# Grouped matmuls in the joined units, four banks for the SSD decays, an earlier SSD tail, half-loaded first units and a per-token final norm

## The reference

```
for i in range(2):
    x = x + 0.5 * swiglu(rmsnorm(x, ffn_norm[i, 0]), w_gate_up[i, 0], w_down[i, 0])
    h = rmsnorm(x, mix_norm[i])
    y = short_conv_mixer(h, ...) if i == 0 else ssd_mixer(h, ...)
    x = x + y
    x = x + memory_cross_attn(rmsnorm(x, xa_norm[i]), rmsnorm(mem, xa_mem_norm[i]), ...)   # 4 heads, 256 memory tokens
    x = x + 0.5 * swiglu(rmsnorm(x, ffn_norm[i, 1]), w_gate_up[i, 1], w_down[i, 1])
return rmsnorm(x, final_norm)
```

## Time and profile before

| | before |
|---|---|
| device time, median of 3 runs (range) | 1339.04 us (1337.76 to 1341.26) |
| device time of the profiled execution | 1343.49 us |
| span of the profiled execution | 1341.7 us |
| PE busy | 1294.3 us (96%) |
| PEld busy | 1169.4 us (87%) |
| DVE busy | 1002.5 us (75%) |
| ACT busy | 756.5 us (56%) |
| POOL busy | 231.6 us (17%) |
| share of the chain that ended last: PE, DVE, ACT | 79%, 10%, 5% |
| granted TensorE clock, mean | 0.991 |

### The profile page before, as it was taken

One profiled execution on the slowest core, in us unless ns is written; L12 is line 12 of the kernel. 1 busy time (PEld: TensorE's weight loads), 2 busy tenths in 40 slices (PEclk: granted clock), 3 DMA queues, 4 the chain that ended last, 5 costly groups with the idle time before them and its releaser, 6 DMA issues.

```text
span 1341.7 us, 24083 instructions
## 1 busy us (share of the span) xinstructions
PE 1294.3 (96%) x8324; PEld 1169.4 (87%) x8324; DVE 1002.5 (75%) x1553; ACT 756.5 (56%) x1362; POOL 231.6 (17%) x316
## 2 busy tenths in 40 slices
PE   6999999999999999999999997999979999999996
PEld 5888889989998888888888885899979999888885
DVE  6887767687768888668887666798856767888764
ACT  6555544356556556446555554678855655655641
POOL 2333111112001111101111100024451201111111
PEclk9999999999999999999999999999999999999998
DMA  6656655545445556645556443344344543555750
GB/s 241 192 187 205 199 167 171 183 157 186 129 142 181 188 183 218 195 146 178 183 187 230 166 167 126 123 149 138 126 142 170 164 149 133 186 182 186 225 192 32
DMA packets 60120, 228.32 MB, mean 170 GB/s; under 512 B 6673, under 2 KB 7953, under 8 KB 59793
## 3 DMA queue, kind: packets, MB, share of 16 engines
q1 hardware_dynamic: 60048, 227.39, 51.8%
HBM read 226.31 MB, written 1.05 MB: 169 GB/s over the span
## 4 chain that ended last, share of the span: by engine, by line
PE 79%; DVE 10%; ACT 5%; issue 3%; POOL 2%; DMA 0%; DVEq 0%; ACTq 0%; SPq 0%; POOLq 0%
PE bank L1175 79%; DVE w_lo L673 3%; ACT w_hi L343 3%; DVE acc L676 2%; DVE decay L943 1%; DVE acc L673 1%; DVE x L673 1%; ACT sq L376 1%; ACT corr L343 1%; POOL ssq L1087 0%; DVE t L673 0%; ACT h L343 0%; POOL y L1156 0%; DMA x<-x_t 0%; POOL root_y L1138 0%
## 5 line engine op out<-in xcount | busy, mean ns | idle before, releaser
L1175 PE MATMUL bank<-h,w_hi 128*128 128x512 f32 (+1 forms) x2056 | 621.3, 365 | 15.5 <-DVE w_lo L673 10.3
L673 DVE TENSOR_TENSOR w_lo<-raw,w_hi 128x1024 fp32r<-128x1024 f32 (+1 forms) x401 | 521.6, 1304 | 54.2 <-ACT w_hi L343 52.7
L1175 PE MATMUL bank<-h,w_lo 128*128 128x256 f32 x1736 | 489.3, 282 | 0.0
L343 ACT ACTIVATE w_hi<-raw 128x1024 fp32r<-128x1024 f32 (+1 forms) x401 | 442.1, 1103 | 45.3 <-PE bank L1175 44.1
L1175 PE MATMUL bank<-a,w_hi 128*128 128x512 f32 (+1 forms) x1664 | 461.2, 348 | 0.2 <-DVE w_lo L673 0.2
L1175 PEld LDWEIGHTS bank<-h,w_hi 128*128 128x128 f32 x2056 | 367.7, 190 | 83.7 <-issue 10.2
L1175 PE MATMUL bank<-a,w_lo 128*128 128x256 f32 x1280 | 360.8, 282 | 0.0
L1175 PEld LDWEIGHTS bank<-h,w_lo 128*128 128x128 f32 x1736 | 330.4, 190 | 0.0
L1175 PEld LDWEIGHTS bank<-a,w_hi 128*128 128x128 f32 x1664 | 290.1, 191 | 42.3 <-issue 0.5
L1175 PEld LDWEIGHTS bank<-a,w_lo 128*128 128x128 f32 x1280 | 243.8, 190 | 0.0
L343 ACT ACTIVATE corr<-bank 128x256 f32<-128x256 f32 x233 | 88.5, 381 | 267.6 <-PE bank L1175 267.6
(11 more groups left out here) (177 smaller groups left out, 1115.6 us busy)
## 6 DMA issues: line engine op xcount, KB each, us to landing
raw<-w_gu SPq DMA_DIRECT2D x176, 512.0 KB, 3.6
raw<-w_down SPq DMA_DIRECT2D x64, 704.0 KB, 4.1
raw<-w_xbc SPq DMA_DIRECT2D x32, 512.0 KB, 3.5
raw<-w_conv_in SPq DMA_DIRECT2D x24, 512.0 KB, 4.1
raw<-w_q SPq DMA_DIRECT2D x16, 512.0 KB, 4.2
raw<-w_k SPq DMA_DIRECT2D x16, 512.0 KB, 4.2
raw<-w_v SPq DMA_DIRECT2D x16, 512.0 KB, 3.6
raw<-w_o SPq DMA_DIRECT2D x16, 512.0 KB, 3.7
```

The lines of the kernel that those rows point to most:

```text
L343: return nc.scalar.activation(out, in_, ACT.Copy, scale=scale)
L673: return nc.vector.tensor_tensor(out, a, b, op)
L1175: return nc.tensor.matmul(out, lhs, rhs, start=start, stop=stop, skip_group_check=check)
```

## The change

Five things are changed.

1. **Order in a joined unit.** `pairs` now takes a range of blocks: first the 512-column matmuls of all of them, then the 256-column ones. Number and shapes stay.
2. **Decays.** Four banks (5, 6, 4, 7) take the place of two, PE's wait is for `diff_ready` j-3, ACT's exps of a step are those of the diffs of the step before, `rows` is finished before the two small exps, and `normed_lo` moves from DVE to POOL.
3. **Tail of the SSD scan.** The formulas become a table (`due`) with exceptions for groups 5 to 7 (`TAIL`), and part of the last eight units is issued ahead of and behind group 7's transposes (`second_halves`).
4. **Start.** x comes in five pieces, the first two units in halves (`half_units`), unit 0 by ACT's queue; five matmuls on `ones` run first; the first norm's sums come after four units, and its root is spread after a fifth; `mem` is loaded later and in four pieces.
5. **End.** x times the final gain is transposed as each tile comes (`turn_final`), and the root is applied per token (per partition) in four 512-column operations by DVE and ACT; four transfers of 256 KB go out in place of eight of 128 KB.

```diff
+HALF_W = UNIT_W // 2
+X_CHUNKS = [(0, 1), (1, 2), (2, 4), (4, 6), (6, 8)]
...
+        DECAY_BANKS = (5, 6, 4, 7)
...
-        SSD_STEPS = 4 * (GROUPS + 3) + 2
         SSD_UNITS = 4 * GROUPS + KT
+        SSD_STEPS = SSD_UNITS + 2
+
+        TAIL = {"y": {7: 35}, "state": {7: 36}, "y_add": {7: 36}, "yo": {6: 34, 7: 36}, "yoff": {6: 35, 7: 37},
+                "square": {6: 36, 7: 38}, "root": {6: 36, 7: 38}, "yn": {5: 35, 6: 37, 7: 39}, "yt": {5: 35, 6: 38, 7: 40}, "a_rest": {5: 36, 6: 39, 7: 40}}
...
         def _(act):
...
+                if f == 0:
+                    corr_copy(0, 0, n0)
+                    corr_copy(1, 1, n0 + 1)
+                    split(n0 + 1 + AHEAD)
+                    for t in range(2, 4):
+                        act.wait_ge(evac[t - 2], 1)
+                        corr_copy(t, t, n0 + t)
+                    split(n0 + 2 + AHEAD)
+                    norm(0)
+                    ffn_post(f, 0, 0, 0, None)
+                    ffn_post(f, 1, 1, 0, a_hi[:, 0, :])
+                    ffn_post(f, 2, 2, 0, None)
...
                         copy(rows[:, :], bank[7][:, 0:SEQ]).then_inc(row_hi, 1)
+                        act.wait_ge(row_rest, 1)
+                        copy(rows[0:2 * H, :], acc[0][0:2 * H, :]).then_inc(row_lo, 1)
                         nc.scalar.activation(e_acum[:, :], d["nacum"][:, 1, :], ACT.Exp, scale=-1.0).then_inc(acum_exp, 1)
                         nc.scalar.activation(dsd[:, :], rest[:, :], ACT.Exp).then_inc(acum_exp, 1)
-                        act.wait_ge(row_rest, 1)
-                        copy(rows[0:2 * H, :], acc[0][0:2 * H, :]).then_inc(row_lo, 1)
...
-                    while lcount < decays_by(s - 1):
+                    while lcount < decays_by(s - 2):
                         decays(lcount)
...
         def _(dve):
...
-                    if 5 < s <= 5 + KT:
-                        normed_lo(s - 6)
...
+            dve.wait_ge(rms_n_ready, SS_INDEX[NORM_FINAL] + 1)
+            dve.wait_ge(turned, 1)
+            for c in range(2):
+                cols = slice(c * 512, c * 512 + 512)
+                nc.vector.tensor_scalar(final[:, 0, cols], bank[FINAL_BANKS[0][c]][:, :], rms_n[:, 0:1], None, ALU.mult).then_inc(out_ready, 1)
...
         def _(pool):
...
+                for k in range(KT):
+                    pool.wait_ge(nhi_ready, k + 1)
+                    nc.gpsimd.tensor_tensor(a_lo[:, H_NORMED + k, :], normed[k], a_hi[:, H_NORMED + k, :].bitcast(F32), ALU.subtract).then_inc(nh_ready, 1)
...
         def _(pe):
...
-            def pairs(out, lh, ll, both, start, stop):
-
-                mm(out[:, :], lh, both, start, False)
-                return mm(out[:, SEQ:], ll, both[:, 0], False, stop)
+            def pairs(out, s, r, ks, k0, start, stop, ready=None):
+
+                for k in ks:
+                    if ready:
+                        pe.wait_ge(*ready(k))
+                    mm(out[:, :], w_hi[s][:, k * P:k * P + P], r[:, :, k0 + k, :], start and k == ks[0], False)
+                for k in ks:
+                    ins = mm(out[:, SEQ:], w_lo[s][:, k * P:k * P + P], r[:, 0, k0 + k, :], False, stop and k == ks[-1])
+                return ins
...
+                if b == 0:
+                    half_units()
+                    one_unit(2, bank[2], KT, 0, h, True, True)
+                    one_unit(3, bank[3], KT, 0, h, True, True)
+                    norm_sums(b)
+                    one_unit(4, free(name, 4), KT, 0, h, True, True)
+                    pe.wait_ge(eye_in, 16)
+                    norm_spread(b)
+                    for t in range(5, 8):
+                        one_unit(t, free(name, t), KT, 0, h, True, True)
+                    return
...
-                at_least(pe, diff_ready, j - 1)
+                at_least(pe, diff_ready, j - 3)
...
-                    ins = mm(bank[5 + j % 2][:, r * SEQ:r * SEQ + SEQ], pick[:, hd:hd + 1].broadcast_to((P, P)), rows[:, :], True, True)
+                    ins = mm(bank[DECAY_BANKS[j % 4]][:, r * SEQ:r * SEQ + SEQ], pick[:, hd:hd + 1].broadcast_to((P, P)), rows[:, :], True, True)
...
+                    if t == SSD_UNITS:
+                        second_halves(range(1), range(KT - 2))
...
+                second_halves(range(1, 3), range(KT - 2))
+                second_halves(range(3), range(KT - 2, KT))
+                second_halves(range(3, KT), range(KT))
...
+            for k in range(KT - 1):
+                turn_final(k)
             norm_sums(NORM_FINAL)
-            norm_spread(NORM_FINAL)
+            turn_final(KT - 1).then_inc(turned, 1)
```

More of the change, by code:

```diff
@@ L317, in load_phase @@
                 else:
-                    with sp.Fori(1, units // SLOTS) as i:
+                    with sp.Fori(3 if name == "gu0" else 1, units // SLOTS) as i:
                         for s in range(SLOTS):
@@ L1408, in wide_unit, with second_halves @@
                     ins.then_inc(unit_done, 1)
+            def second_halves(ks, part):
+                for k in ks:
+                    out = bank[k] if k < 4 else free("ssd_out", k)
+                    unit(first["xbc"] + SSD_UNITS + k, half(out, k), KT, KT, a, False, True,
+                         ready=(yt_ready, 0) if k == 0 else None, check=True, part=part)
             def ssd():
@@ L1505, in ssd @@
                         ins.then_inc(xt_done, 1)
-                for k in range(KT):
-                    out = bank[k] if k < 4 else free("ssd_out", k)
-                    unit(nx + SSD_UNITS + k, half(out, k), KT, KT, a, False, True,
-                         ready=(yt_ready, 0) if k == 0 else None, check=True)
+                second_halves(range(1, 3), range(KT - 2))
+                second_halves(range(3), range(KT - 2, KT))
+                second_halves(range(3, KT), range(KT))
             pe.wait_ge(ones_set, 1)
-            pe.wait_ge(gain_in, 16)
+            for i in range(5):
+                mm(bank[7][:, 0:SEQ], ones[:, :], ones[:, 0:1].broadcast_to((P, SEQ)), True, True)
             ffn(0)
```

302 lines of the change are left out of this document (188 added, 114 removed).

## The result

The changed kernel took 1319.92 us (median of 4 runs, 1319.54 to 1320.69) beside 1340.15 us (1337.76 to 1341.81) for the kernel before: a ratio of 0.985, with a 95% interval of 0.9833 to 0.9867. It is 20 us faster. The forecast was 1304 with a range from 1295 to 1317: the direction was right, the time lies 3 us above the range, and of 34.8 us forecast 20.2 came.

What follows compares the result with a forecast made beforehand. PE was taken to bound the kernel. Grouping -10.5, decays -15, SSD tail -9, start +1, openings +1.2 and end -2.5 sum to -34.8, from a median of 1339.04 to 1304 us; 8 in 10 from 1295 to 1317.

Steps and rivals of the forecast that it cites:

- What bounds the kernel: Whole kernel: PE, busy 96% of a 1341.7 us span and 79% of the chain, so time comes only from PE.
- Decays: Ten z steps: exp leaves the ring, PE sets the step, 47.7 us towards 31.0; -15 us (-16.7 to -9).
- rival (b): z steps: POOL slows two DVE operations, DVE becomes the limit; -9 in place of -15, 1310 us; chance 0.13.
- Grouping: Joined units: a wide and narrow pair falls from 0.3535 to 0.3487 us, 2200 pairs; -10.5 us (-15 to -2).
- the openings: Openings of gu1 to gu3: narrow matmuls come behind the last wide one while PE waits for h; +1.2 us (0 to 2.5).
- the bound set: Sign in gu, down and o units: a whole grouped unit of eight blocks at 2.79 us or less is right.
- SSD tail: SSD scan's end: group 7's 7.83 us stall and half clock go, group 5 stalls 1.5; -9 us (-10.5 to -7.5).
- Start: Kernel start: first matmul 3.3 us earlier, but norm sums and root later, unit 6 near 31.8; +1 us (-1.5 to +3.5).
- End: Output: root used at once, fewer wider operations on DVE and ACT, doubled transfers; -2.5 us (-3.2 to -1.8).
- Rival (a): Joined units: matmul order is worth nothing, the pair stays at 0.354 us; 1315 us; chance 0.22.

Runs made afterwards that it cites:

- the third: Repaired kernel (three repairs to the changed kernel, 1308.4 us) with grouped units two by two, two wide matmuls then two narrow: 1307.2 us (1306.4 to 1308.0).

## Why the prediction was wrong, step by step

**What bounds the kernel: right.** Every gain and loss was one of PE's stretches.

**Decays: right.** -15 forecast (-16.7 at best), -16.4 in the phase and -17.1 measured alone. PE sets the step and DVE does not; the fear that POOL would slow it there (rival (b)) did not come true, and the move of `normed_lo` was needed for nothing.

**Grouping: the step that failed most.** Forecast -10.5 (ends -2 and -15) and, with the openings, -9.3; alone it measured 0 (0.9999, 0.9986 to 1.0012), and undoing it gained 2 to 4. Two things went wrong, and neither is the price of a grouped unit, which came as computed (2.79 us, the bound set was 2.79).

The first is the price before. I took 0.3535 per pair from the profiled execution and called the 0.347 rare. It is rare in that execution, which was also the slowest of the runs of the kernel before, 4.45 us above the median. I wrote that down as a difference of the execution and subtracted it from both sides. But if a run differs by the spells of its lower level, 4.45 us are 4.45 / 0.0066 = 670 pairs more at the lower level in a median run, on which grouping loses 3 ns each in place of winning 4. Of a steady gain of 9 us that leaves 4.5. That the two levels exist and change within a run is shown, and that the clock does not make the spread; that the levels make up all of it was only reckoned, since there is one trace of each kernel. The profile with grouping alone fits: 4.0 us shorter in the phases of joined units than the profile of the kernel before, which lies 4.45 above its median.

The second is the openings. I gave 1.2 us to two places. By the phases the gu1 opening cost 2.5 (+1.03 in place of a gain of 1.46), gu3 0.9, and conv_out, which I had not looked at, 1.1 (+0.8 in place of a gain of 0.3): 4.5. In gu1 some 1.6 of the 2.5 is the clock, since gu3 with the same stall and no half clock lost 0.9. That the order in these places is the cause is shown: alternating there alone brought 3.8 us back. I had also read the earlier trace rows too coarsely: of the three waits on `h`, 4.8 us together, the longest (1.88, at 298.96) is that of the first attention, whose units are not joined, so gu1 (1.45) and gu3 (1.48) were the two places, and their price was 0.9 with the clock up. Together the two things would make the zero: 9 less 4.5 less 4.5.

**SSD tail: half right.** Forecast -9, found -3.8. The long wait went as said, and the next one was named: group 5's transposes. Its size was off, 2.6 for 1.5, because `yn` was taken at the 0.62 it has when POOL is idle, though the change itself puts POOL's work beside it. I had the row that shows it and used it for the z steps alone. And I had given the new stall no price for the clock, 3.2 us, though I had put 2.9 on the old one. These two, 1.1 and 3.2, are most of the 5.2 that the term fell short.

**Start: within its bounds, at the upper end.** Forecast +1 (-1.5 to +3.5), measured +2.9. Unit 6 began at 32.22, forecast 31.8, and the half clock behind it, which I had left in the upper end, came.

**End: size off.** Forecast -2.5. From the last matmul of down3 to the end of the span it was 12.87 us (1328.84 to 1341.7) and is 11.40 (1306.80 to 1318.2): -1.5. DVE is done as soon as forecast (1.41 us behind the root), but the transfers end 4.1 us behind it in place of 3.0; I had given the doubled ones up to 0.4 more (with the whole of it the forecast's own sum is 1339.5, -2.2). The rows of the end (DVE, then the last issue):

```profile
1312.70 1.41 DVE L1158 TENSOR_SCALAR final<-bank,rms_n 128x512 f32<-128x512 f32 x2
...
1314.35 0.46 SPq L364 DMA_DIRECT2D out_t<-final  x1
```

**The sum.** Measured by themselves: -17.1 for the decays, 0 for grouping with its openings, +2.9 for the start; by the phases -3.8 for the tail and -1.5 for the end: -19.5, against 20.2 measured. Against the forecast's 34.8 that is 9.3 less from grouping and openings, 5.2 from the tail, 1.9 from the start and 1 from the end, and 2.1 more from the decays.

**Rival (a)** gave 1315 for a grouping that is worth nothing, with a chance of 0.22. Its term came out, nothing for grouping, but not for its reason. The Trainium skill ("TensorE: Matmul & The Clock Gate", section "Wait — 56ns, not 53.3ns?") gives each matmul its columns at 2.4 GHz and a fixed 2.5 ns or so, which leaves order no part in it. The runs have 347 or 353 ns for one order, 349 for the other and 0.7 less (124.08 - 123.82 over 352 pairs) for the third in the gu phases: small differences, but not none, and none of them the 325 that an estimate from the page's figures gives.

## What to carry to other kernels

When a profiled execution lies 0.3% above the median, ask which of its stretches is slower than in another run before taking a price per instruction from it: an edit that acts on that very price may already be half there in the median. Where a change fills or moves a wait, price what stands behind it twice, once for the wait and once for the clock; and look at which operations of DVE and POOL on whole tiles now fall together. A matmul order that waits for its input block by block should do all the work of a block as it comes (3.8 us here), whatever order is best elsewhere.

## What the runs showed of the hardware

One order of matmuls has two speeds. Alternating 512 and 256 columns at a granted clock of 1.00, ten pairs took 3.53 us and 3.47 us in one execution, in spells of up to 1100 pairs in the kernel before; starts follow one another in a cycle of three pairs (241, 120, 236, 113, 233, 117 ns) at the upper level and of two (233, 117, 231, 113 ns) at the lower. What sets which was not found.

The half clock behind a stall is no fixed price. The wait of 2.56 to 2.58 us on group 5's `y` was followed by it in five profiles (3.2 us lost in four, 4.6 in one, against the sixth) and in one by none. The wait of 1.87 to 1.90 us in the first attention's opening was followed by it in seven of fourteen. The waits of 1.45 to 1.49 us in gu1's alternating opening were followed by it in none of seven profiles; the grouped ones of 2.17 to 2.20 in seven of seven in gu1, yet in one of seven in gu3, where they are as long.

POOL's operations on a tile stretched a DVE operation beside them from 0.62 to 2.13 us, more than threefold.
